# U rows and V rows of a PEER layer, spread over a block's points by weights of their own

## The reference, cut to what matters

```python
    q = (ht @ w_q).reshape(t, PEER_HEADS, PEER_QDIM)
    s1, s2 = ...                       # scores against 128 + 128 sub-keys per head
    v1, i1 = lax.top_k(s1, PEER_TOPK)
    v2, i2 = lax.top_k(s2, PEER_TOPK)
    best, ci = lax.top_k(cand, PEER_TOPK)
    experts = e1 * N_KEYS + e2
    gates = jax.nn.softmax(best, axis=-1)
    ...
        u = u_table[eb]
        act = jax.nn.gelu(jnp.einsum('thkd,td->thk', u, xb)) * gb
        vv = v_table[eb]
        return jnp.einsum('thk,thkd->td', act, vv)
```

## Time and profile before

| what | value |
|---|---|
| median of three runs | 3499.28 us |
| the profiled execution, time | 3493.39 us |
| the profiled execution, span | 3491.7 us |
| PE busy | 2338.5 us (67%) |
| VectorE (DVE) busy | 2343.0 us (67%) |
| ScalarE (ACT) busy | 857.8 us (25%) |
| GpSimd (POOL) busy | 2264.7 us (65%) |
| DMA, mean | 363 GB/s |

### The profile page before, as it was taken

One profiled execution on the slowest core, in us unless ns is written; L12 is line 12 of the kernel. 1 busy time (PEld: TensorE's weight loads), 2 busy tenths in 40 slices (PEclk: granted clock), 3 DMA queues, 4 the chain that ended last, 5 costly groups with the idle time before them and its releaser, 6 DMA issues.

```text
span 3491.7 us, 46932 instructions
## 1 busy us (share of the span) xinstructions
PE 2338.5 (67%) x16321; PEld 1420.7 (41%) x16321; DVE 2343.0 (67%) x5605; ACT 857.8 (25%) x2418; POOL 2264.7 (65%) x2091
## 2 busy tenths in 40 slices
PE   7673546886837858767758858768847783444477
PEld 6563424654614535434525536534624450000011
DVE  4539878677797687767788687767687668444400
ACT  4320112332213123313214223314213321111122
POOL 1003775656657767677777767677677777777675
PEclk9886567997968869978869869888858895555555
DMA  7734898999989999999999999999999999999999
GB/s 240 248 119 164 303 352 308 377 366 356 338 286 383 410 358 413 407 401 398 408 360 393 410 356 413 411 399 405 408 372 382 408 409 368 398 409 409 409 402 370
DMA packets 392252, 1267.89 MB, mean 363 GB/s; under 512 B 43789, under 2 KB 95058, under 8 KB 382802
## 3 DMA queue, kind: packets, MB, share of 16 engines
q0 software_dynamic: 294912, 1073.87, 79.3%
q1 hardware_dynamic: 78674, 149.06, 11.7%
q10 hardware_dynamic: 18432, 41.95, 3.3%
HBM read 1225.89 MB, written 38.83 MB: 362 GB/s over the span
## 4 chain that ended last, share of the span: by engine, by line
DVE 22%; PE 22%; POOL 22%; DMA 20%; issue 8%; ACT 3%; DVEq 2%; ACTq 1%; SPq 0%; POOLq 0%
PE zz L1553 13%; DMA v_ring<-in_peer_v,idxT 11%; POOL u_ring L701 11%; POOL v_ring L716 9%; DVE u_ring L1102 7%; DMA u_ring<-in_peer_u,idx 6%; PE va L1553 3%; PE rr L1553 2%; DMA u_ring<-in_peer_v,idxT 2%; PE ox L1553 1%; DVE work L1438 1%; DVE work L1440 1%; DVE work L1383 1%; DVE work L1377 1%; POOL u_ring L716 1%
## 5 line engine op out<-in xcount | busy, mean ns | idle before, releaser
L701 POOL DMA_INDIRECT u_ring<-in_peer_u,idx x1024 | 1169.8, 1142 | 771.0 <-issue 285.1
L716 POOL DMA_INDIRECT v_ring<-in_peer_v,idxT x960 | 1025.7, 1068 | 412.1 <-issue 240.3
L1102 DVE SCALAR_TENSOR_TENSOR u_ring<-u_ring,hn_t 128x1024 f32<-128x1024 f32 x896 | 1067.5, 1222 | 213.2 <-DMA u_ring<-in_peer_u,idx 207.2
L1553 PE MATMUL va<-v_ring,column 128*32 128x256 f32 x7680 | 743.4, 490 | 616.6 <-DMA v_ring<-in_peer_v,idxT 572.2
L1553 PE MATMUL zz<-work 128*128 128x256 f32 (+3 forms) x3008 | 668.0, 382 | 58.3 <-DVE work L1284 17.9
L1553 PEld LDWEIGHTS va<-v_ring,column 128*32 128x32 f32 x7680 | 195.2, 123 | 1099.7 <-DMA v_ring<-in_peer_v,idxT 897.2
L1553 PEld LDWEIGHTS zz<-work 128*128 128x128 f32 (+1 forms) x3008 | 495.9, 207 | 253.2 <-issue 135.1
L780 ACT ACTIVATE column<-onehot,wT 128x32 f32<-128x32 f32 x1024 | 285.6, 315 | 790.7 <-PE va L1553 759.0
L1102 DVE SCALAR_TENSOR_TENSOR u_ring<-u_ring,zz 128x1024 f32<-128x1024 f32 x128 | 156.2, 1221 | 169.9 <-DMA u_ring<-in_peer_u,idx 169.9
L1553 PE MATMUL rr<-work,later 128*128 128x512 f32 x144 | 99.0, 808 | 47.7 <-DVE work L1303 34.6
L1553 PE MATMUL zz<-work,w_q_t 128*128 128x128 f32 x1024 | 130.8, 291 | 0.0
(11 more groups left out here) (301 smaller groups left out, 2637.0 us busy)
## 6 DMA issues: line engine op xcount, KB each, us to landing
work<-d_w SPq DMA_DIRECT2D x42, 1024.0 KB, 7.9
work<-in_w_out ACTq DMA_DIRECT2D x64, 512.0 KB, 10.7
u_ring<-in_peer_u,idx POOLq DMA_INDIRECT x1024
v_ring<-in_peer_v,idxT POOLq DMA_INDIRECT x960
work<-d_kT SPq DMA_DIRECT2D x36, 256.0 KB, 8.3
work<-d_v SPq DMA_DIRECT2D x36, 256.0 KB, 6.8
w_q_t<-in_peer_w_q SPq DMA_DIRECT2D x1, 8192.0 KB, 25.6
work<-d_subT SPq DMA_DIRECT2D x8, 1024.0 KB, 8.5
```

Of the source, the lines that this page charges most:

```text
L701: g.indirect_dma_start(u_ring[:, n % RU, :], None, u_rows, bass.IndirectOffsetOnAxis(idx[b % 2][:, s:s + 1], 0)).then_inc(u_landed[n % RU] ...
L716: g.indirect_dma_start(v_row(n), None, v_rows, bass.IndirectOffsetOnAxis(idxT[b % 3][:, t:t + 1], 0)).then_inc(v_landed[slot] if slot < RV ...
L1102: v.scalar_tensor_tensor(u_ring[:, m % RU, :], u_ring[:, m % RU, :], 1.0, token, ALU.mult, ALU.mult, accum_out=dots[:, s:s + 1]).then_inc( ...
L1553: return t_.matmul(out_, lhsT, rhs, start=start, stop=stop, skip_group_check=True)
```

## The change

`points()` yields two weights per point, one for U rows and one for V rows, taken from a list SHARES by stage and by place in the stage. MARKS is replaced by PACE, a pair of counts at each block's end. Between two ends the U rows run with the sum of the U weights and the V rows with the sum of the V weights. In block 1 the U rows of block 0 are done by 0.60 of the block instead of 0.62, and the V rows run from there to the block's end. The pace at the ends of blocks 1 to 7 was (128, 40), (250, 118), (339, 207), (500, 368), (593, 461), (756, 624), (884, 750), and is (128, 28), (250, 118), (341, 207), (498, 366), (593, 463), (760, 626), (884, 752).

```diff
--- before.py
+++ after.py
@@ -128,43 +128,76 @@
     return any(0 <= m < NCH and needs_tokens(m) for m in (n - 7, n - 8))
 
 
+SHARES = {"start": ((6, 6, 6), (7.2, 6, 6)),
+          "level": ((6, 6, 5.9, 6, 6), (6, 6, 6, 6, 8.2)),
+          "state": ((7, 7), (7, 9.8)),
+          "key": ((9, 9, 9), (9, 9, 9)),
+          "mix": ((7.1,), (8,)),
+          "out": ((10.8, 10), (7, 10)),
+          "hn": ((8,), (9.3,)),
+          "pq": ((10, 9.8, 10, 10), (10, 15.9, 10, 10)),
+          "score": ((7.9,), (29.7,)),
+          "top": ((7, 7, 7, 8.5, 7), (7, 7, 7, 11, 7)),
+          "p": ((5, 7.1, 5, 2.5), (5, 5.3, 5, 2.5))}
+FREE_BANK = {"start": 0, "level": 0, "state": None, "key": 1, "mix": 1, "out": 1, "hn": None, "pq": 1, "score": 1, "top": 1}
+
+
+def shares(name, k, count):
+
+    u, v = SHARES[name]
+    if name == "key":
+        i = 0 if k == 0 else 2 if k == count - 1 else 1
+    elif name == "p":
+        i = 0 if k < 4 else 3 if k >= NCH else 1 if k < GV_END else 2
+    else:
+        i = k
+    return u[i], v[i]
+
+
 def points():
 
 
     for b in range(1, NB):
         if segment_before(b) is not None:
             for n in range(NCH + 9):
-                yield ("p", segment_before(b), n), 5.0 if n < NCH else 2.5, None if n < 4 or token_turn_pending(n) else 1
-        for name, count, weight, free in (("start", 3, 6.0, 0), ("level", 5, 6.0, 0), ("state", 2, 7.0, None),
-                                          ("key", b + 1, 9.0, 1), ("mix", 1, 8.0, 1), ("out", 2, 10.0, 1), ("hn", 1, 8.0, None),
-                                          ("pq", 4, 10.0, 1), ("score", 1, 8.0, 1), ("top", 5, 7.0, 1)):
+                yield ("p", segment_before(b), n), *shares("p", n, 0), None if n < 4 or token_turn_pending(n) else 1
+        for name, count in (("start", 3), ("level", 5), ("state", 2), ("key", b + 1), ("mix", 1), ("out", 2), ("hn", 1),
+                            ("pq", 4), ("score", 1), ("top", 5)):
             for k in range(count):
-                yield (name, b, k), weight, free
-
-
-
-MARKS = [(1, 0.62, 128, 0), (1, 1.0, 128, 40), (2, 1.0, 250, 118), (4, 1.0, 500, 368), (6, 1.0, 756, 624), (7, 1.0, 884, 750)]
+                yield (name, b, k), *shares(name, k, count), FREE_BANK[name]
+
+
+
+PACE = {1: (128, 28), 2: (250, 118), 3: (341, 207), 4: (498, 366), 5: (593, 463), 6: (760, 626), 7: (884, 752)}
+FIRST = 0.60
 
 
 def table():
 
 
-    names, at, free, ends = [], [], [], {0: 0.0}
-    x = 0.0
-    for name, weight, bank in points():
-        x += weight
+    names, wu, wv, free, last = [], [], [], [], {}
+    for name, a, c, bank in points():
         names.append(name)
-        at.append(x)
+        wu.append(a)
+        wv.append(c)
         free.append(bank)
         if name[0] == "top" and name[2] == 4:
-            ends[name[1]] = x
-    marks = [(0.0, 0, 0)] + [(ends[b - 1] + share * (ends[b] - ends[b - 1]), u, v) for b, share, u, v in MARKS]
+            last[name[1]] = len(names)
     u, v = [], []
-    for x in at:
-        (x0, u0, v0), (x1, u1, v1) = next((p, q) for p, q in zip(marks, marks[1:]) if x <= q[0])
-        share = (x - x0) / (x1 - x0)
-        u.append(min(int(u0 + share * (u1 - u0)), SLOTS * next(b for b in ends if x <= ends[b])))
-        v.append(int(v0 + share * (v1 - v0)))
+    i0 = u0 = v0 = 0
+    for b, (u1, v1) in PACE.items():
+        su, sv = sum(wu[i0:last[b]]), sum(wv[i0:last[b]])
+        x = y = 0.0
+        for i in range(i0, last[b]):
+            x += wu[i] / su
+            y += wv[i] / sv
+            if b == 1:
+                u.append(min(int(u1 * x / FIRST + 1e-6), u1))
+                v.append(int(v1 * max(0.0, (x - FIRST) / (1 - FIRST)) + 1e-6))
+            else:
+                u.append(min(int(u0 + (u1 - u0) * x + 1e-6), SLOTS * b))
+                v.append(int(v0 + (v1 - v0) * y + 1e-6))
+        i0, u0, v0 = last[b], u1, v1
     k = 0
     while v[-1] < SLOTS * (NB + 1):
         u.append(min(u[-1] + 2, SLOTS * NB))
```

## The result

The changed kernel takes 3452.72 us (median of 4 runs, 3449.35 to 3458.29), the kernel before 3498.49 us beside it (4 runs). The ratio is 0.9868, with a 95% interval of 0.9852 to 0.9884: 46 us or 1.3% faster, where I had forecast 21 us and a range of 3458 to 3502 us. The profiled execution after took 3458.29 us (span 3456.4), 5.6 above its median; that of before lies 5 under its own. So the two traces differ by 35 us, not by 46.

The account below looks back on a forecast made before the run. Gather transfers bound the kernel, their total time taken as fixed, so only DMA idle time could shrink. Blocks 1 to 2 gave -6, (d) -11, (e) -4: -21 us, from 3499.28 to 3478 us, range 3458 to 3502.

Parts of the forecast that it names:

- Only the two row counts change: Whole kernel: no instruction, ring, semaphore or DMA added or removed; only row counts per point and GpSimd's order change.
- (a): Block 1's top: with fewer V rows the index is turned near 614 us, not 620.50; -6.3 us, bounds 0 and -8.
- (b): Segment 1's projection: eight more dots in the convolution steps load VectorE; +3 us, bounds 0 and +9.8.
- (c): Block 2: six fewer dots on VectorE, ten more V rows; -3 us, bounds -7.3 and +2.
- (d): Tops of blocks 3 and 5: idle transfer time shrinks 7.7 us, a later index turn costs 2.1; net -5.6 us each.
- (e): Tops of blocks 4 and 6: more V rows fill idle time, GpSimd issuing 45 gathers at most; -2 us each.
- The rule weighed there: Tops: GpSimd's DMA issue starves during VectorE's two-port operations; if in force, the gains of (d) and (e) would be nothing.
- (f): Key to hn of blocks 3 to 7: rows moved to the tops shorten these transfer-bound stretches, some 5 us each.
- (g): Projections of segments 2 and 3: 9 and 11 more U rows covered by transfers; 0 us, bounds up to +11 and +13.
- the idle time only moves: First rival: gaps filled in tops reopen elsewhere, or GpSimd cannot issue the extra rows; 3497 us, chance 0.13.
- slower by dots: Second rival: 28 more dots in the projections' convolution steps lengthen VectorE's chain; +22 us, 3521 us, chance 0.11.
- The third: Third rival, better than forecast: all lower bounds together, -44 us, 3455 us, chance 0.16.

Follow-up runs that it names:

- run 14: The changed kernel with the marks of blocks 3 to 7 back at their old values: 3470.41 us, ratio 0.9917 to the kernel before.
- run 16: The changed kernel itself, measured again beside others of its set: 3452.53 us, ratio 0.9871 to the kernel before.
- run 1: The changed kernel with all old marks and FIRST 0.62, so only the new weights are left: 3483.78 us, ratio 0.9951 to the kernel before.
- run 13: The changed kernel with 40 V rows at block 1's end and FIRST 0.62, late marks new: 3463.23 us, ratio 0.9903 to the kernel before.
- run 10: The changed kernel with only the marks of blocks 4 and 6 old: ratio 0.9872 to the kernel before.
- run 17: The changed kernel with the marks of blocks 6 and 7 old, on the slower kind of chip: ratio 0.9932 to the kernel before.
- run 18: The changed kernel with the marks of blocks 3 to 5 old, on the slower kind of chip: ratio 0.9879 to the kernel before.
- run 4: The kernel before with one number changed, 28 V rows in place of 40 at block 1's end: 3490.05 us, ratio 0.9979 to the kernel before.
- run 3: The changed kernel with 40 V rows in place of 28 at block 1's end: 3461.25 us, ratio 0.9902 to the kernel before.
- run 2: The changed kernel with the old weights for both kinds of row, only the marks new: 3485.94 us, ratio 0.9972 to the kernel before.
- run 6: The changed kernel with the old weights for U rows, V weights and marks new: ratio 0.9887 to the kernel before.
- run 8: The changed kernel itself, measured again on another chip: ratio 0.9876 to the kernel before.
- run 9: The changed kernel with all marks of blocks 3 to 7 old, on the slower kind of chip: ratio 0.9888 to the kernel before.

## Why the prediction was wrong

The sign and the mechanism in the tops were right, the size was less than half: 21 us forecast, 46 measured. The step of its sum that failed is a term put at nothing, the late marks. On the terms of its sum:

- **A term was missing.** The prediction weighed the weights and block 1's mark and gave the marks of blocks 3 to 7 no line of their own; the transfer time was "fixed", so that rows moved between full stretches were an even exchange, 1.28 us each. Runs 14 and 16, and 1 and 13, show 16 to 17 us there. This is the larger part of the 25 us by which the forecast missed. What makes it so large is shown only as far as stretches go: with the new weights, gathers taken out of the stretch to block 4's end and out of block 7 save 2 to 3 us each, those added in between cost 0.7 to 1.8 (table 2). The division of this worth over the marks is open (runs 10, 17, 18).
- **"Only the two row counts change"** isn't so. `table()` works out from them also where a block's activation (GELU), its transpose (TURN) and its last step come. By the two tables, block 2's activation moves from step 21 of segment 2's projection to step 17 and block 4's from step 23 of segment 3's to step 18. The late marks alone move block 4's from 19 to 18 and block 5's from block 7's first level point to its last start point, and end the tail one point sooner. In the stretch to block 4's end, where 11.5 and 13.3 us are saved, they move none of these. No run holds these places apart from the rows, so their part in the 16 us is untested.
- **"A fixed transfer time"** failed as well: of the 41.5 us between the copies of the two traces some 12 are packets that took less time, not idle time.
- **(a) Block 1's handover, -6.3.** The handover shrank by 12.3 us, from 12.45 (608.05 to 620.50) to 0.15: twice the forecast. The main step that failed is that xT would still come at 609.90, 1.85 us behind the index. It came 2.74 us ahead of it, which makes 4.6 of the 6 us missed; the other 1.5 are the six rows, 2.80 us at a granted clock of 1.00 for 4.26 at 0.64. The copies had been late because of V rows: four columns on ScalarE stood ahead of the x copies, which began 605.63 - 602.69 = 2.9 us after the transposes had ended. With fewer V rows the copies start while the second half is still being transposed (603.53, before 605.19). VectorE's own part of block 1 became 3.5 us shorter too (index ready 287.4 us after the copy of block 0 before, 284.0 after). Yet 16 us in block 1 were worth 7 to the end (run 4), 12 in the changed kernel (run 3): table 1 reads block 1's change as 14 gathers not made (+1.8 beyond), and the gain stands one interval on, where 13 gathers more cost 1.6 us. By block 2's end, at equal gathers, 14 us are gained (run 4). So the number -6 was near run 4's 7 us by luck: the local gain was double, and where the rest of it went isn't shown.
- **(b) Segment 1's projection, +3.** Its convolution steps are 8.7 us longer, near the upper bound, but not a loss: they hold 10 gathers more, 12.8 us of transfers, and went from a share of 0.99 and 381 GB/s to 1.02 and 407. It was charged as a cost of VectorE; it is work brought forward, in part into idle transfer time.
- **(c) Block 2, -3.** From 226.5 to 222.7 us: -3.8. The number is right; all of it lies in key to hn (72.6 to 68.8 us), where the plan has two dots fewer, 2.4 us. That the dots are the reason isn't shown.
- **(d), (e) The tops, -7.7 and -2 of idle time for each.** Foreseen 19.4 us of idle time, measured 18.8; for blocks 3 and 5 -6.2 each, for 4 and 6 -3.3 and -3.1. Runs 1 and 2 tie it to the weights. The wait on L804 was to be about 15 us and is 15.74. The +2.1 us charged for the index being turned late did not come: PE waits 0.86 and 1.92 us for its last rows, and then it is VectorE's index that it waits for (L1480). But the two stages are 3.0 and 2.8 us longer than before, with VectorE busy 63.0 for 60.4 us in block 3.
- **(e) GpSimd as the limit**, 45 gathers at most in such a top: it issued 49, one in 1.34 us where 1.43 had been taken. Its gathers beside a busy VectorE took 1.03 (V) and 1.14 us (U) in place of 1.15 and 1.19. The limit was put too low, though GpSimd is nearly at it.
- **The rule weighed there.** The Trainium skill (SBUF — State Buffer, the box on "DVE blocks DMA") warns of starving while VectorE runs an operation in its two-port mode. With VectorE busy 59.39 of 65.80 us this trace has no sign of starving; which of its operations run in that mode, if any, no run here tells, so the rule itself wasn't put to the test.
- **(f) Key to hn of blocks 3 to 7, some 5 us shorter each.** Cut at the plan's points they are 5.6, 6.7, 0.1, 3.2 and 13.7 us shorter: about right in sum, not one by one.
- **(g) Segments 2 and 3, 0.** Right in total: the convolution stretches grew by 9.2 and 15.5 us at an unchanged share of 1.03, where their 5 and 11 gathers more are 6.4 and 14.1 us.

The terms as measured, against the kernel before: the weights 17 us (run 1), block 1's mark 7 (run 4), the late marks 16 (run 14 against 16); 40 of the 46. Of these the prediction had the first two, at 15 and 6. Runs 1 and 4 are measured from the kernel before, the late marks from the changed one, so this sum mixes two bases. The rest of 6 us is within what four medians with intervals of some 5 us each leave open; the worth of block 1's mark is larger (12) in the changed kernel than in the old one, and so the parts support each other somewhat.

Of the rivals, "the idle time only moves" falls (it fell by 30 us), and so does "slower by dots" (the convolution stretches grew by their transfers alone, and run 6 isn't faster). The third, the lower ends together at 3455 us, was nearest, but not by its terms.

## What to carry to other kernels

Where one resource is full and the work on it is dealt out by a plan, a mark that moves four items is a term of the sum like any other: don't put it at nothing because the moves cancel at the rate of a full stretch. Prices taken from two plans didn't foretell a third either (runs 17 and 18, on the other kind of chip), so the whole plan has to be measured. See also what else a table decides: here the places of the activation and of the transpose moved with the counts. Read a stage's gain only after taking out the work that it no longer holds; block 1's 16 us were 14 gathers not made. And when a wait is to go, follow what the waiting engine's partner had queued ahead of its part: with the columns on ScalarE no longer in the way, 4.6 of the 12.3 us at block 1's end were gained.

## What the runs showed of the hardware

Chips differ in what the gathers move. Windows of 200 us of the tail, where only gathers run beside their sums: the changed kernel in run 16, then in run 8.

```profile
3000.00:3200.00 200.00, 84.32 (x624) 15.77 (x624) 96.17 (x157) 25.07 (x78) 150.40 (x161) 0.50 1.03 409
```

```profile
3150.00:3350.00 200.00, 95.18 (x572) 28.78 (x564) 89.33 (x146) 20.85 (x71) 130.59 (x140) 0.54 0.99 373
```

409 GB/s against 373, 161 gathers against 140, and whole programs of 3497 against 3722 us, while a dot product takes 1.22 us and a gather 0.93 us of GpSimd (150.40 / 161 and 130.59 / 140) on both. Between two executions of one kernel on one chip the time varies by 8 to 10 us either way (3488 to 3506 over 24 runs), so that a change of 7 us, as in run 4, took ten runs to tell; on the slower kind it varies by more (3700 to 3746 over 23), which is why runs 9 and 10 tell so little. And the transfers' own time isn't fixed: the same 1267.9 MB took 3291 to 3312 us of 16 engines on the chips of the faster kind. The five traces with the new weights and the new late marks lie at 3291 to 3297 us, the other five at 3299 to 3312. Why a packet takes longer in one plan than in another, no run here tells, nor why the chips differ.
